# Leaving out the products of constants ahead of the last two passes of each expert loop

## The reference, cut to what matters

```python
def one_block(args):
    tok, w, e = args
    xb = x_pad[tok]
    hb = jax.nn.silu(xb @ wg[e]) * (xb @ wu[e])
    return (hb @ wd[e]) * w[:, None]
...
shared = (jax.nn.silu(x @ swg) * (x @ swu)) @ swd
return (routed + shared).reshape(B, S, D)
```

## Time and profile before

| | |
|---|---|
| median of 3 runs | 1451.43 us (1450.06 to 1452.11) |
| profiled execution | 1450.41 us |
| its span, first to last instruction | 1448.6 us |
| tensor engine busy | 1411.7 us (97%), 8416 matmul records |
| vector engine busy | 437.6 us (30%) |
| scalar engine busy | 316.8 us (22%) |
| moved by DMA | 509.54 MB, mean 352 GB/s over the span |
| mean granted tensor clock | 0.998 |

### The profile page before, as it was taken

One profiled execution on the slowest core, in us unless ns is written; L12 is line 12 of the kernel. 1 busy time (PEld: TensorE's weight loads), 2 busy tenths in 40 slices (PEclk: granted clock), 3 DMA queues, 4 the chain that ended last, 5 costly groups with the idle time before them and its releaser, 6 DMA issues.

```text
span 1448.6 us, 21041 instructions
## 1 busy us (share of the span) xinstructions
PE 1411.7 (97%) x8416; PEld 720.6 (50%) x8416; DVE 437.6 (30%) x1161; ACT 316.8 (22%) x746; POOL 48.0 (3%) x86
## 2 busy tenths in 40 slices
PE   7999999999999999999999999999999999999997
PEld 3345656444444445444565456564444444444454
DVE  1146435312122212121345243442122222222123
ACT  2134322111111111111345122411111111111112
POOL 0100301000000000000100010010000000000000
PEclk9999999999999999999999999999999999999999
DMA  9999528999999999999962246299999999999991
GB/s 392 382 384 426 223 85 333 392 399 424 410 427 424 421 426 425 425 425 425 402 249 116 116 160 239 88 379 394 405 423 421 423 414 426 425 426 424 424 404 60
DMA packets 49603, 509.54 MB, mean 352 GB/s; under 512 B 5872, under 2 KB 6272, under 8 KB 10432
## 3 DMA queue, kind: packets, MB, share of 16 engines
q1 hardware_dynamic: 29328, 370.42, 61.6%
q10 hardware_dynamic: 16416, 119.54, 20.1%
q0 software_dynamic: 3760, 18.20, 3.3%
HBM read 499.10 MB, written 11.01 MB: 352 GB/s over the span
## 4 chain that ended last, share of the span: by engine, by line
PE 87%; DMA 5%; DVE 3%; ACT 3%; issue 1%; ACTq 0%; SPq 0%; DVEq 0%
PE bank L2056 25%; PE banks L2108 13%; PE banks L1956 10%; PE banks L443 5%; DMA s_dn_ring<-in_moe_wd_dram 4%; PE ybank L1984 3%; PE banks L1120 3%; PE banks L1984 3%; PE bank L1986 3%; PE bank L505 2%; PE ybank L1748 1%; PE banks L1748 1%; PE bank L424 1%; DMA s_gu_ring<-in_ada_w_dram 1%; PE banks L698 1%; PE banks L1125 1%
## 5 line engine op out<-in xcount | busy, mean ns | idle before, releaser
L2056 PE MATMUL bank<-s_gu_ring,s_hbuf 128*32 128x512 f32 (+1 forms) x2688 | 395.2, 593 | 0.9 <-DVE s_hbuf L2189 0.9
L2056 PEld LDWEIGHTS bank<-s_gu_ring,s_hbuf 128*32 128x32 f32 (+1 forms) x2688 | 121.1, 119 | 263.3 <-issue 262.8
L2108 PE MATMUL banks<-s_dn_ring,s_hTs 128*32 128x512 f32 (+1 forms) x1344 | 204.2, 596 | 0.9 <-DMA s_dn_ring<-in_moe_wd_dram 0.9
L2234 DVE TENSOR_TENSOR s_ylo<-banks,s_yhi 128x512 fp32r<-128x512 f32 x112 | 77.5, 692 | 321.3 <-ACT s_yhi L2150 321.3
L1956 PE MATMUL banks<-s_sel,s_htok 128*128 128x512 f32 (+1 forms) x640 | 144.8, 374 | 0.5 <-issue 0.5
L1956 PEld LDWEIGHTS banks<-s_sel,s_htok 128*128 128x128 f32 x640 | 106.2, 188 | 60.7 <-issue 44.3
L2150 ACT CAST s_yhi<-banks 128x512 fp32r<-128x512 f32 x112 | 65.6, 586 | 297.6 <-PE banks L2108 297.6
L2229 DVE SCALAR_TENSOR_TENSOR s_hh<-s_sg,s_wsl,bank 128x256 f32<-128x256 f32 x56 | 26.9, 481 | 302.7 <-ACT s_sg L2141 302.7
L2108 PEld LDWEIGHTS banks<-s_dn_ring,s_hTs 128*32 128x32 f32 (+1 forms) x1344 | 56.3, 118 | 118.7 <-issue 118.0
L2141 ACT ACTIVATE s_sg<-bank 128x256 f32<-128x256 f32 x56 | 21.5, 384 | 379.4 <-PE bank L2056 379.4
L2189 DVE COPY s_hbuf<-banks 128x512 f32<-128x512 f32 (+1 forms) x60 | 39.4, 656 | 96.0 <-PE banks L1956 96.0
(11 more groups left out here) (463 smaller groups left out, 1482.7 us busy)
## 6 DMA issues: line engine op xcount, KB each, us to landing
s_gu_ring<-in_moe_up_dram SPq DMA_DIRECT2D x124, 2048.0 KB, 16.1
s_dn_ring<-in_moe_wd_dram ACTq DMA_DIRECT2D x114, 1024.0 KB, 16.3
s_gu_ring<-in_ada_w_dram SPq DMA_DIRECT2D x24, 2048.0 KB, 14.2
s_dn_ring<-in_moe_wd_dram SPq DMA_DIRECT2D x14, 1024.0 KB, 11.4
s_gu_ring<-in_win_dram SPq DMA_DIRECT2D x6, 2048.0 KB, 11.9
s_gu_ring<-in_moe_up_dram SPq DMA_DIRECT2D x8, 1024.0 KB, 10.2
s_gu_ring<-in_wqkv_dram SPq DMA_DIRECT2D x6, 1024.0 KB, 19.4
s_gu_ring<-in_wo_dram SPq DMA_DIRECT2D x2, 2048.0 KB, 20.3
```

The costliest lines, as they stand in the source:

```text
L2056: last = pe.matmul(W0[o:o + n, :], tokens_of(p, k)[:, o:o + n], w[:, k, :, :], start=(k == 0), stop=(k == KC - 1))
L2108: last = pe.matmul((W1, W2)[half][o:o + n, :], hTs[:, f, o:o + n], dn_ring[:, DN_PLACE[dn_of[(l, r)][0]], w0:w0 + 512], start=(f == 0), st ...
L2234: dve.tensor_tensor(ylo[:, half, :], (W1, W2)[half], yhi[:, half, :].bitcast(F32), ALU.subtract).then_inc(S["y_low"], 1)
```

## The change

The call of `keep_awake` ahead of the last two passes of each layer's expert loop is taken out. Nothing else is touched.

```diff
@@ -2045,8 +2045,6 @@
                             pe.wait_ge(S["wall_full"], l * NB + q + 1)
                         if l * NP + p:
                             pe.wait_ge(S["hT_full"], l * NP + p)
-                        if p >= NP - 2:
-                            keep_awake(pe, W0, (8, 24)[p - NP + 2])
                         for r in ranks:
                             s, n, _ = gu_of[(l, r)]
                             pe.wait_ge(slot_in[s].h, n)
```

## The result

| | before | changed |
|---|---|---|
| median | 1450.89 us (7 executions, 1450.06 to 1452.11) | 1440.73 us (7 executions, 1438.58 to 1446.03) |
| profiled execution | 1450.41 us, span 1448.6 | 1445.37 us, span 1443.6 |
| mean granted tensor clock, profiled | 0.998 | 0.995 |

A forecast was written before the change was run, and what follows sets the result against it. The prediction took tensor engine and transfers to be in balance in the expert loops. Its terms, 2 x 0 + 2 x 5.56 = 11.1 us, came off 1451.43 to give 1440.3 us, range 1438.5 to 1446.0.

The forecast's parts named there:

- The sum: Whole kernel: 2 x 0 + 2 x 5.56 = 11.1 us off 1451.43, giving 1440.3 us.
- term of 5.56 us a layer: Ahead of pass 27 in each layer: the 24 removed products come off the path whole, 5.56 us.
- The 8 are hidden by a landing: Ahead of pass 26: the 1.98 us a layer removed turns into idling before the down weights land; gain booked 0.
- Next in line is the last gate/up load: Ahead of pass 27: its last gate/up weights land 1.7 and 1.4 us before the new start, so no wait.
- The landing stays where it is: Pass 26's third down weights still land at 1404.95 and 690.19; nothing removed releases their load earlier.
- No fall of the clock: In the hole of about 2.4 us ahead of pass 26's down products, the granted clock stays at 1.00.
- rival (a): Clock falls in pass 26's hole, back within the down products: 3.6 us a layer, 1447.5 us; chance 0.07.
- The price of a fall: Behind pass 26's hole, work at 1.2 GHz takes double time: 3.64 us of down products, +3.6 us a layer.
- (b): Clock stays low to the end of pass 27's gate/up products: 5.1 us lost a layer, 1461.7 us; chance 0.04.

## Why the prediction was right, and where not

**The sum.** 1440.3 us forecast, 1440.73 measured. The gain was forecast at 11.1 us and came out at 10.2; the base, the median of three executions, was 1451.43 us where seven give 1450.89. These two errors, 0.9 and 0.5 us, partly cancel in the time. The sum's term of 5.56 us a layer holds and is a little small. Without a fall the gain is 11.5 us by the fastest executions (1450.06 to 1438.58); the trace with 4 products in the hole has layer 1's pass 27 11.49 us ahead, 0.20 of it from the first pass on. Each layer gives 0.14 us more than worked out, and it stands in one place: from the start of pass 26's down products to the start of pass 27's gate/up products, after that work, it is 3.43 us with the same 32 records (690.08 to 693.51 in that trace), where it was 3.57 to the first constant in the earlier trace rows. The constants began 0.14 us later than gate/up products do in their place.

**The 8 are hidden by a landing.** Right: down products of pass 26 at 690.37 in the changed kernel against 690.33, and the holes of about 2.4 us. The run with the early down load shows the other side: the landing was the cover, and once it is earlier, the 8 cost about 2 us (2.1 by the medians, 1.8 by the spans).

**Next in line is the last gate/up load, with 1.4 to 1.7 us to spare.** Right: no wait ahead of pass 27's gate/up products in the changed kernel, and a wait of 1.21 and 0.55 us once they could start some 2.4 us earlier.

**The landing stays where it is.** Right only on average. It moved by nearly 2 us between executions of the same code: 690.2 in before, 692.1 with the 8 kept, and in layer 1 a transfer of 27.47 instead of 26.21 us. The prediction had one reading of each landing and treated it as fixed. The late landing made the hole 3.71 us in one case. Why the landings move is open; no run here tells that apart.

**No fall of the clock.** This step failed. I argued that 2.44 us is shorter than any idling that had lost the clock, with the nearest lost one behind the last product, and gave rival (a) 0.07. In the changed kernel the profiled execution lost the clock in both holes, and another took as long; of the kernel with the 8 left out alone ten of eleven executions took 2.0 to 5.2 us more than the fastest. The trace of before showed a gap of 0.88 us that kept the clock and an idling of over 3.5 us that lost it, and nothing between; with a hole in that stretch the two outcomes should have had about even chances. That the median came out so near the forecast is partly luck: the base was 0.5 us too high, the gain without a fall was some 0.4 us larger than forecast, and the losses took 1.3 us of it by the medians. The median execution lies 2.2 us above the fastest one. A fall in one hole, a fall in the linear attention or a late landing would each fit that; it has no trace, and which it was is not shown.

**The price of a fall.** Also mis-sized, the other way: (a) had 3.6 us a layer, the down products at half speed from end to end. The rows show about 3.4 us at the low level, which is 1.7 us of work lost, and the down products take 1.70 us more. Where a part of the low stretch lay in the hole, the loss was a little smaller: 1.54 us with the 8 left out alone, layer 0. In these five cases the work behind a fall doesn't set its price; the time that the clock stays low does. So (b) didn't come true either: in no trace did the clock stay low to the end of pass 27's gate/up products, and no kernel here with the 24 left out was slower than before.

The page "TensorE: Matmul & The Clock Gate" of the Trainium skill, in "HAM oscillation — how this bites in real kernels", was set beside the forecast as speaking against it: a wait for a transfer between bursts of products lets the clock fall, and the next burst starts cold; in its example these waits are about 3 to 5 us long. By the 5.34 us of pass 26's down products the traces agree, and they show it for shorter waits too, of 2.41 to 2.62 us, though in three of five cases the first 0.2 to 0.5 us of the burst still ran at the higher level.

## What to carry to other kernels

Products that only keep an engine busy have two prices, and they must be read apart: ahead of work whose data is there they cost their whole length (24 of them: 5.7 us a layer here), ahead of work that waits for a transfer they cost nothing and may save the clock (8 of them: 1.5 to 1.7 us for each fall avoided). Before such products are judged, find the landing behind them; and better than filling a wait is to end it, by issuing the one late load in the other queue, ahead of loads with time to spare, which came out 3.2 us under the kernel that keeps the 8, timed in the same group. Where a median moves by some microseconds and executions scatter by as many, look at the mean granted clock of each, but count the falls in a trace: 0.995 stood apart from 0.998 here, while 0.997 did not say whether one had been lost.

## What the runs showed of the hardware

- A hole of 2.4 to 3.7 us ahead of the down products lost the clock in all five profiled cases. It need not do so in every execution: with the 8 left out alone, one of eleven took 1450.14 us with a clock of 0.999; it has no trace. Holes of 0.41 to 1.70 us lost nothing in seven cases.
- The fall doesn't wait for the work to begin again, nor does it come at a fixed point. Twice the clock went low in the last 0.1 to 0.3 us of the hole (at 692.09 us with the 8 kept, at 690.17 with the 8 left out, both layer 0), and three times 0.2 to 0.5 us after the products had started (690.83 and 1404.24 in the changed kernel, 1406.87 with the 8 left out). Each time it stayed low for 3.4 us and cost 1.5 to 1.7 us.
- The clock can fall with little idling: at the end of the linear attention, between 877 and 883 us, behind a stretch of transposes and small products with one gap of 0.62 us. The changed kernel, the one with the 8 kept and the one with layer 0's constants alone left out lost it there in the profiled execution. The profile of before, with the same instructions and the same gap, did not, nor did the other five. One such fall cost 1.65 us. It fits the 2 us over which the executions of before scatter, but that wasn't tested, and why it falls in some executions only is open.
- A transfer of 1 MB behind a full queue, in the same place of both loops, took 26.1 to 26.4 us from issue to landing in eleven of fourteen cases and 27.2 to 28.3 us in three. Issued by sync instead, in the kernel with the early load, it took 20.4 and 19.4 us.
